# Output projection in three token passes, and the branch placed behind the first gather of a mixture-of-experts layer

## The reference, cut to what matters

```
x = x + merged @ w_out                       # merged: gated sum of the two mixers, (T, 2048)
h = rms_norm(x, g_ffn)
grp_prob = softmax(t @ w_router_group)       # 4 groups, top 1
g_p, g_i = top_k(grp_prob, 1)
sel_logits = router_expert logits of the chosen group        # 4 experts
e_p, e_i = top_k(softmax(sel_logits), 2)
w = g_p * (e_p / sum(e_p))
combine = sum(one_hot(expert_id, 16) * w)    # (T, 16)
hid = silu(t @ w_gate_e) * (t @ w_up_e)      # per expert, 512 wide
out = (hid * combine) @ w_down_e
y = x + out
```

## Time and profile before

| what | value |
|---|---|
| executions (3) | 1939.7, 1942.26, 2071.72 us |
| median | 1942.26 us |
| profiled execution | 1940.69 us |
| its span, slowest core (core 1) | 1939.1 us |
| spans of the 8 cores | 1922.6 to 1939.1 us |
| TensorE busy / VectorE busy / ScalarE busy | 86% / 42% / 38% of the span |
| projection, from first to last matmul (L1304) | 1207.6 to 1351.4 us |
| first matmul of the gather (L1464), of the experts (L1529) | 1407.85 us, 1433.26 us |

### The profile page before, as it was taken

One profiled execution on the slowest core, in us unless ns is written; L12 is line 12 of the kernel. 1 busy time (PEld: TensorE's weight loads), 2 busy tenths in 40 slices (PEclk: granted clock), 3 DMA queues, 4 the chain that ended last, 5 costly groups with the idle time before them and its releaser, 6 DMA issues.

```text
span 1939.1 us, 30864 instructions; the slowest of 8 cores (1922.6 to 1939.1 us)
## 1 busy us (share of the span) xinstructions
PE 1664.2 (86%) x11342; PEld 1072.2 (55%) x11342; DVE 820.7 (42%) x1244; ACT 743.0 (38%) x1246; POOL 143.5 (7%) x283
## 2 busy tenths in 40 slices
PE   2775777889998988879999999998588899898995
PEld 1542344566566566454444444887466676666662
DVE  3634334434434443421211212233435567665765
ACT  4654446556665655671111110032331322323221
POOL 0010100200201200001111100000000000010000
PEclk9887888899999999989999999999789999999997
DMA  9469891895995999546998972851139789798796
GB/s 255 170 101 115 104 122 23 105 115 68 121 113 70 123 121 117 114 66 110 138 121 120 141 98 53 245 122 66 25 71 244 163 208 234 179 216 207 193 236 212
DMA packets 57084, 263.09 MB, mean 136 GB/s; under 512 B 10464, under 2 KB 10720, under 8 KB 49312
## 3 DMA queue, kind: packets, MB, share of 16 engines
q0 software_dynamic: 27168, 152.06, 57.7%
q1 hardware_dynamic: 29760, 108.96, 17.2%
HBM read 404.65 MB, written 73.40 MB: 247 GB/s over the span
## 4 chain that ended last, share of the span: by engine, by line
PE 72%; DVE 9%; ACT 7%; issue 5%; DMA 4%; SPq 1%; DVEq 0%; ACTq 0%
PE psum L1116 11%; PE psum L586 11%; PE psum L1529 10%; PE psum L607 6%; PE psum L1121 6%; PE psum L1304 6%; PE psum L1565 5%; PE psum L933 4%; PE psum L915 4%; DMA arena<-wbf 3%; PE psum L1551 3%; PE psum L1464 2%; DVE arena L1473 2%; DVE arena L921 1%; DVE arena L559 1%
## 5 line engine op out<-in xcount | busy, mean ns | idle before, releaser
L586 PE MATMUL psum<-arena 128*128 128x512 bf16 (+1 forms) x1072 | 286.7, 403 | 13.6 <-DVE arena L559 13.5
L1529 PE MATMUL psum<-arena 128*128 128x256 bf16 x2048 | 243.7, 273 | 5.8 <-DMA arena<-wbf 5.8
L1529 PEld LDWEIGHTS psum<-arena 128*128 128x128 bf16 x2048 | 199.8, 98 | 55.9 <-issue 8.3
L1116 PE MATMUL psum<-arena 128*128 128x512 bf16 x1024 | 226.2, 379 | 0.0
L926 ACT ACTIVATE arena<-psum 128x512 bf16<-128x512 f32 x352 | 197.9, 592 | 34.8 <-PE psum L915 33.3
L933 PE MATMUL psum<-arena 128*128 128x256 bf16 x832 | 164.6, 280 | 49.9 <-ACT arena L923 41.9
L586 PEld LDWEIGHTS psum<-arena 128*128 128x128 bf16 x1072 | 106.8, 103 | 121.1 <-issue 50.9
L1116 PEld LDWEIGHTS psum<-arena 128*128 128x128 bf16 x1024 | 100.2, 98 | 120.6
L915 PE MATMUL psum<-arena 78*128 78x256 bf16 x832 | 166.0, 281 | 0.0
L1554 DVE TENSOR_TENSOR arena<-psum,arena 128x1024 f32<-128x1024 f32 x128 | 153.8, 1221 | 10.2 <-PE psum L1551 4.0
L559 DVE SCALAR_TENSOR_TENSOR arena<-psum,arena 64x512 bf16<-64x512 f32 (+3 forms) x121 | 89.4, 739 | 144.1 <-ACT arena L556 136.6
(11 more groups left out here) (152 smaller groups left out, 1831.1 us busy)
## 6 DMA issues: line engine op xcount, KB each, us to landing
wbf<-wexp POOLq DMA_DIRECT2D x108, 512.0 KB, 36.1
arena<-wbf SPq DMA_DIRECT2D x108, 512.0 KB, 12.6
arena<-wexp POOLq DMA_DIRECT2D x84, 512.0 KB, 10.5
arena<-win POOLq DMA_DIRECT2D x58, 512.0 KB, 9.3
arena<-xs SPq DMA_DIRECT2D x24, 1024.0 KB, 8.3
arena<-wobf SPq DMA_DIRECT2D x14, 1024.0 KB, 6.0
wobf<-wo POOLq DMA_DIRECT2D x8, 1024.0 KB, 57.4
arena<-wup POOLq DMA_DIRECT2D x16, 512.0 KB, 11.8
```

The costliest lines, as they stand in the source:

```text
L586: prog.add("pe", lambda e, k=k: e.matmul(PS(bank, 0, n), lhsT=wslot[s][:, k, :], rhs=src[:, k, lo:lo + n], start=(k == 0), stop=(k == 15)) ...
L1116: prog.add("pe", lambda e, k=k, bank=bank, wt=wt, tl=tl: e.matmul(PS(bank), lhsT=wt[:, k, :], rhs=hTo[:, k, tl:tl + 512], start=(k == 0), ...
L1529: prog.add("pe", lambda e, k=k, f=f, bank=bank, Wv=Wv: e.matmul(PS(bank, f * 256, f * 256 + 256), lhsT=Wv[:, k, :], rhs=X[:, k, e4 * 256:( ...
```

## The change

Four things are changed.

1. The projection has three passes: tiles 0 to 3, 4 and 5, 6 and 7. The slices are taken in the orders 0..7, 5 6 7 0..4 and 2..7 0 1, so each later pass begins with the three slices that the one before left. A third buffer `woslot[2]` lies on ring buffers 4 and 5. `load_wo` now names its buffer; 18 loads in all.
2. `side` holds tiles 0 to 5 (43 pieces, one of them a barrier), spread over the 32 groups of passes 1 and 2: `slot_no * nside / 31` says how many have to be out behind each group. Tiles 4 and 5 have scratch buffers of their own (`h2f_b`, `h2Tf_b`) on ring buffers 0 to 3. The tail holds tiles 6 and 7.
3. Since ring buffers 0 to 5 are in use, `load_slice(0..6)` is issued behind the last pass, behind a barrier; GpSimd's one-element copy is gone.
4. `build_P(0)` stands straight behind `pos`; the combine weights and their split come behind it, then `gather(0)` and `oprep(0)`, and only then the branch. The small routing tiles move out of the memory of `P` into that of `hid` for it.

```diff
-    B_wo = [Buf("wo%d" % i) for i in range(NWO)]
+    woslot.append(R3.alloc([128, 16, 256], BF16, at=16384))
+    B_wo = [Buf("wo%d" % i) for i in range(3)]
...
-    rt_small = [R3.alloc([128, 8, 16], F32) for _ in range(7)]
+    rt_small = [R3.alloc([128, 8, 16], F32, at=off_hidend - 4096 + i * 512) for i in range(7)]
...
+    h2f_b = R3.alloc([128, D], F32, at=0)
+    h2Tf_b = R3.alloc([128, 16, 128], F32, at=8192)
...
+    wo_seq = list(range(8)) + [0, 1, 2, 3, 4] + [5, 6, 7, 0, 1]
+    wo_at = {}
+
+    def load_wo(s):
+        if wo_seq:
+            n = wo_seq.pop(0)
+            wo_at[n] = s
+            prog.add("sp", lambda e: e.dma_start(out=woslot[s].rearrange("p a b -> p (a b)"), in_=wobf_d[n]),
+                     reads=[B_convo[3 if n < 4 else 7]], writes=[B_wo[s]], dsem=S_wo[s])
...
-    for t in range(4):
-        side.append(lambda t=t: part1(t, h2f_a, B_h2f_a))
+    for t in range(6):
+        hf, Bhf, hT_, BhT_ = (h2f_a, B_h2f_a, h2Tf_a, B_h2Tf_a) if t < 4 else (h2f_b, B_h2f_b, h2Tf_b, B_h2Tf_b)
+        if t == 4:
+            side.append(lambda: barrier([B_h2f_a], B_h2[4:6]))
+        side.append(lambda t=t, hf=hf, Bhf=Bhf: part1(t, hf, Bhf))
         if t:
-            side.append(lambda t=t: router(t - 1, h2Tf_a, B_h2Tf_a, 6))
-        else:
-            side.append(lambda: None)
+            hp, Bhp = (h2Tf_a, B_h2Tf_a) if t <= 4 else (h2Tf_b, B_h2Tf_b)
+            side.append(lambda t=t, hp=hp, Bhp=Bhp: router(t - 1, hp, Bhp, 6))
...
-    for pas in range(2):
+    for pas, (t_lo, t_hi) in enumerate(((0, 4), (4, 6), (6, 8))):
         nb = 8 if pas == 0 else 4
         for ci in range(8):
-            cg = ci if pas == 0 else (ci + 6) % 8
-            s = ci % NWO
-            for t4 in range(4):
-                t = pas * 4 + t4
+            cg = (ci + (0, 5, 2)[pas]) % 8
+            s = wo_at[cg]
+            for t in range(t_lo, t_hi):
...
-                if pas == 1 and side:
-                    side.pop(0)()
-            if pas == 1 or ci < 6:
-                load_wo()
+                if pas >= 1:
+                    slot_no[0] += 1
+                    while side and nside - len(side) < slot_no[0] * nside / 31.0:
+                        side.pop(0)()
+            if ci < 5:
+                load_wo(s)
...
-        if pas == 0:
-            prog.add("pool", lambda e: e.tensor_copy(out=flag_m[0:1, 0:1], in_=x1[0:1, 7, 0:1]),
-                     reads=[B_x1[7]], writes=[B_flag])
-            for i in range(7):
-                load_slice(i)
-    barrier(B_merged + [B_h2f_a, B_h2Tf_a], B_h2f + B_h2Tf + B_h2[4:8])
-    part1(4, h2f[0], B_h2f[0])
     while side:
         side.pop(0)()
-    for t in range(4, 8):
+    barrier([B_wo[2], B_h2f_b, B_h2Tf_b], B_ring[0:7])
+    for i in range(7):
+        load_slice(i)
+    barrier(B_merged + [B_h2Tf_a], B_h2f + B_h2Tf + B_h2[6:8])
+    part1(6, h2f[0], B_h2f[0])
+    for t in range(6, 8):
...
-    S_y = new_sem()
-    B_y = Buf("y")
-    prog.branch_at(flag_i[0:1, 0:1], B_flag)
-
...
+    build_P(0)
+    dv(lambda e: e.tensor_tensor(out=dsl, in0=sl, in1=l1.to_broadcast([128, 8, 4]), op=ALU.subtract))
+    prog.add("act", lambda e: e.activation(out=ex, in_=dsl, func=AF.Exp), reads=[B_rts], writes=[B_rts])
...
+    dv(lambda e: e.tensor_copy(out=wv[:, :, :, 2], in_=r2), R_, W_)
+    barrier([B_rts, B_wsp], [b for bb in B_hid for b in bb])
+    gather(0)
+    oprep(0)
+    S_y = new_sem()
+    B_y = Buf("y")
+    prog.branch_at(flag_i[0:1, 0:1], B_flag)
...
-    build_P(0)
-    gather(0)
-    oprep(0)
```

More of the change, by code:

```diff
@@ L1097, in build_program @@
     woslot = [R3.alloc([128, 16, 256], BF16) for _ in range(NWO)]
-    B_wo = [Buf("wo%d" % i) for i in range(NWO)]
-    S_wo = [new_sem() for _ in range(NWO)]
+    woslot.append(R3.alloc([128, 16, 256], BF16, at=16384))
+    B_wo = [Buf("wo%d" % i) for i in range(3)]
+    S_wo = [new_sem() for _ in range(3)]
     assert R3.off <= R3.size
-    barrier(all_attn_bufs, B_merged + B_sga + B_sgb + B_tmul + B_wo)
+    barrier(all_attn_bufs, B_merged + B_sga + B_sgb + B_tmul + B_wo[0:2])
     first = [True]
@@ L1178, in build_program @@
     B_L = Buf("L")
-    rt_small = [R3.alloc([128, 8, 16], F32) for _ in range(7)]
-    B_rts = Buf("rts")
     assert R3.off <= off_wo + 3 * 8192
@@ L1215, in build_program @@
     B_h2f_a, B_h2Tf_a = Buf("h2fa"), Buf("h2Tfa")
-    barrier(B_gs + B_sga + B_sgb + B_tmul, B_ring + [B_gbc2])
+    h2f_b = R3.alloc([128, D], F32, at=0)
+    h2Tf_b = R3.alloc([128, 16, 128], F32, at=8192)
+    B_h2f_b, B_h2Tf_b = Buf("h2fb"), Buf("h2Tfb")
+    barrier(B_gs + B_sga + B_sgb + B_tmul, B_ring + [B_gbc2, B_wo[2], B_h2f_b, B_h2Tf_b])
     barrier(B_attn_swa + B_attn_moba, B_h2 + [B_h2f_a, B_h2Tf_a])
     barrier(all_attn_bufs, [B_wr] + B_LT + [B_L, B_comb, B_M, B_pos, B_ones, B_wsp, B_flag, B_rts] + B_ss2l + B_sg + B_wsl)
[L1219 to L1227, removed]
-    load_wo()
-    load_wo()
+    wo_seq = list(range(8)) + [0, 1, 2, 3, 4] + [5, 6, 7, 0, 1]
[6 more added lines that the diff above has]
+                     reads=[B_convo[3 if n < 4 else 7]], writes=[B_wo[s]], dsem=S_wo[s])
+    load_wo(0)
+    load_wo(1)
     prog.add("sp", lambda e: e.dma_start(out=gbc2, in_=gffn_bc[:, :]), writes=[B_gbc2], dsem=S_gbc2)
@@ L1232, in build_program @@
              writes=[B_wr], dsem=S_wr)
+    load_wo(2)
     prog.add("dve", lambda e: e.memset(ss2, 0.0), writes=B_ss2l)
@@ L1280, in build_program @@
     side = []
[L1281 to L1282 removed]
+    for t in range(6):
[3 more added lines that the diff above has]
+        side.append(lambda t=t, hf=hf, Bhf=Bhf: part1(t, hf, Bhf))
         if t:
[L1284 to L1286 removed]
+            hp, Bhp = (h2Tf_a, B_h2Tf_a) if t <= 4 else (h2Tf_b, B_h2Tf_b)
+            side.append(lambda t=t, hp=hp, Bhp=Bhp: router(t - 1, hp, Bhp, 6))
         for q4 in range(4):
[L1288 removed]
+            side.append(lambda t=t, q4=q4, hf=hf, Bhf=Bhf, hT_=hT_, BhT_=BhT_: part2(t, q4, hf, Bhf, hT_, BhT_, 4 + q4 % 2))
         if t:
             side.append(lambda t=t: router_back(t - 1, 7))
[L1291 to L1292 removed]
+    side.append(lambda: router(5, h2Tf_b, B_h2Tf_b, 6))
+    side.append(lambda: router_back(5, 7))
+    nside = len(side)
+    slot_no = [0]
     ob2 = [0]
[L1294 removed]
+    for pas, (t_lo, t_hi) in enumerate(((0, 4), (4, 6), (6, 8))):
         nb = 8 if pas == 0 else 4
         for ci in range(8):
[L1297 to L1300 removed]
+            cg = (ci + (0, 5, 2)[pas]) % 8
+            s = wo_at[cg]
+            for t in range(t_lo, t_hi):
                 bank = ob2[0] % nb
@@ L1414, in build_program @@
              reads=[B_ps[0], B_M], writes=[B_pos])
[L1415 to L1435, removed]
-    S_y = new_sem()
-    B_y = Buf("y")
-    prog.branch_at(flag_i[0:1, 0:1], B_flag)
-    barrier(B_wo + B_merged + [B_gbc2, B_wr, B_L, B_rts, B_wsp] + B_LT + B_h2f + B_h2Tf,
-            B_X + [b for bb in B_Y for b in bb] + B_O + [B_P] + [b for bb in B_hid for b in bb] +
-            [B_wr] + B_LT + [B_L, B_rts])
+    barrier(B_wo + B_merged + [B_gbc2, B_wr, B_L, B_rts] + B_LT + B_h2f + B_h2Tf,
+            B_X + [b for bb in B_Y for b in bb] + B_O + [B_P])
     pb = [0]
```

24 lines of the change are left out of this document (20 added, 4 removed).

## The result

The changed kernel takes 1928.91 us in the median of 4 executions (1928.37 to 1930.53). Its ratio to the kernel before is 0.9939, 95% interval 0.9915 to 0.9963. Measured again on another occasion beside more executions of the kernel before (median 1938.65 of 11) it is 0.9932, interval 0.9914 to 0.995. So it is faster by 0.6%, some 12 us, which the interval tells apart from nothing. The forecast was 1931 us, 11.5 us under before. In some executions of these kernels the cores of one or both dies showed a lower granted clock and the time was up to 10% longer; ratios are taken from the others alone.

A forecast was written before the change was run, and what follows sets the result against it. TensorE's chain bounds the projection, short ScalarE and VectorE steps the tail and routing; what counts is how early the experts start. -7.3 + 11.5 + 2.9 - 15.5 - 3.1 = -11.5 us: forecast 1931 us, range 1920 to 1945.

The forecast's parts named there:

- the step from the sum to what a measurement would tell: Whole kernel: a measurement tells about 2% (39 us) from no change; within that 0.97, faster 0.01, slower 0.02.
- the wait at the first transposes: Start of pass 1: TensorE waits for VectorE's scaling of the first tile, +2.9 us; +4.6 if the clock drops too.
- The wait in pass 0: Projection, pass 0: the wait for a `w_out` slice goes once expert slices are issued later, -7.3 us.
- Rival C: Pass 0: residual tiles and `w_out` slices alone cause the wait, so it stays; time 1938, chance 0.08.
- The slices in passes 1 and 2: Passes 1 and 2: five slices loaded per pass land in time, 11.3 us available against 5.9 us; cost 0.
- Rival A: Passes 1 and 2: slices arrive too slowly and starve them, deciding from 6.8 us a load; slower than before, chance 0.07.
- Two more tiles: Projection passes: side work of two more tiles costs TensorE 5.75 us a tile, +11.5 us.
- The tail, -15.5: Tail behind the projection: two tiles instead of four take 20.5 us instead of 35.96, -15.5 us.
- The early gather, -8.3, the stop +3.5, the clock +1.7: Routing to experts: gather starts 8.3 us earlier, TensorE stops 3.5 us at the branch, then loses 1.7 to slow clock.
- Rivals B and D: Branch ahead of the experts: B, TensorE loses 11 us, time 1938, chance 0.12; D, it loses nothing, 1926, chance 0.12.
- My cancelling of the late weights against the table load: Gather: weights delay VectorE about 1.2 us, ScalarE's first copy loses a 1.28 us table load; length stays 25.4 us.
- The expert slices: Behind the projection: slices issued at about 1360 have some 60 us and need 18.9 us each; cost 0.

The follow-up runs named there:

- late_slices: The kernel before with one edit: the seven expert slices are issued behind the last pass instead of the first; ratio to the kernel before 0.9967.
- side_four: The changed kernel with side work for tiles 0 to 3 only, tiles 4 to 7 in the tail; ratio to the kernel before 0.9947.
- gap: The changed kernel with two empty pieces behind the first piece of side work, ahead of the first transposes; ratio to the kernel before 0.9914.
- passes_only: The changed kernel with its fourth part undone: combine weights and branch ahead of the one-hot again, three passes kept; ratio to the kernel before 0.9955.
- branch_only: The kernel before with the fourth part alone: one-hot behind the positions, weights beside the gather, branch behind it; ratio to the kernel before 0.9978.
- no_branch: The changed kernel without the branch and the second program, leaving out the case of an overflowing expert; ratio to the kernel before 0.9918.
- gap_busy_pe: The changed kernel with two empty pieces behind the first side work and 64 + 28 unread matmuls on TensorE during routing; ratio to the kernel before 0.9927.
- branch_after_onehot: The changed kernel with the branch between one-hot and gather and the combine weights spread over the gather; two executions, 1916.99 and 1923.11 us, no ratio.

## Why the prediction was right or wrong, step by step

The time (1931 forecast, 1928.9 measured, range 1920 to 1945) and the path to it came out as forecast, but two steps of the prediction failed.

The first is the step from the sum to what a measurement would tell. I put at 2% (39 us) the least change that can be told from none, with no row behind it, and so gave 0.97 to "within", although my own sum said 11.5 us. The interval of the ratio, 0.9915 to 0.9963, is 0.24% to either side and lies wholly under 1, and the second measurement has 0.9914 to 0.995: the change is a gain that can be told. The 2 to 3 us by which the fast executions shown before differed, which the prediction used for the lower end of its range, were the better measure.

The second is a term of the sum: the wait at the first transposes, +2.9, cost 4.7 us (step 3 below).

On core 1, from the first projection matmul to the first expert matmul, the change takes 12.25 us (225.7 to 213.4) off; the forecast for that way was 13.2.

1. *The wait in pass 0, -7.3.* Shown: pass 0 has no hole any more, and `late_slices` removes 7.0 us with that line alone. Rival C falls: without the expert slices the wait is gone on three cores and down to 0.2 to 0.6 us on four. Core 3 keeps 2.8 us, so a small part of the wait can have another cause on some core.
2. *The slices in passes 1 and 2, 0.* Shown on all cores of the changed kernel's profile. Ten loads landed in 4.9 us each, inside a window of 11.3:

```profile
arena<-wobf SPq DMA_DIRECT2D x10, 1024.0 KB, 4.9
```

Rival A decides from 6.8 us on, so it falls.

3. *Two more tiles, +11.5.* Shown by `side_four`, 11.4. *The wait at the first transposes, +2.9*: this is the term that was sized wrong. The wait itself was 2.94 us, but I took the clock to stay up behind it and kept the fall for the upper end of the range. On core 1 it falls, and `gap`, which takes the wait away, shows the step to cost 4.7 us. The upper end (4.6) was the right value there; on cores 0, 3 and 5 the clock stayed up, and the 2.9 was right.
4. *The tail, -15.5.* Measured -16.6, so this term was 1.1 short. I took the start of the old tail as it was; the second tile's transposes come 0.8 us sooner (11.2 us in, not 11.95), because ScalarE no longer has a third tile between them (in the kernel before it begins to square that tile at 1362.83, ahead of the second tile's first copy at 1365.41), and the two routers run without a break (64 passes in 7.17 us).
5. *The early gather, -8.3, the stop +3.5, the clock +1.7.* Shown: -8.3, +3.65 and +1.4 on core 1 (15.53 - 14.14), confirmed by `passes_only`, `branch_only` and `no_branch`. Rivals B and D fall with them: the branch costs TensorE what it cost VectorE, neither 11 us nor nothing. The rule of the Trainium skill that spoke against the change ("Runtime: NRT & Kernel Launch", Instruction fetch mechanics) fits the stop; that it is a fetch no run here shows. The 108 ns of "Advanced Engine Details and Errata", Control Flow Timing, is not what an engine loses here (3.65 us). My cancelling of the late weights against the table load also held on core 1: the gather itself, without the stop, is 28.94 - 3.65 = 25.3 us against 25.4 before. But `gap_busy_pe` shows that it held only because the clock was low.

The expert slices are the place where I was lucky rather than right. I gave them 60 us and a need of 18.9. Issued from 1361.7 on, and the last two from 1381.0, the nine of them took 12.2 us each to land (median) and kept the DMA engines busy to about 1391; the experts start at 1421, so the slack was some 30 us. Stretches of core 1:

```profile
1370.00:1380.00 10.00, 9.29 (x81) 8.52 (x79) 2.80 (x7) 5.02 (x5) 0.00 (x0) 1.00 1.03 179
...
1380.00:1390.00 10.00, 0.42 (x3) 0.24 (x3) 5.97 (x33) 0.23 (x1) 1.07 (x2) 0.65 1.03 191
...
1390.00:1395.00 5.00, 2.85 (x14) 2.03 (x15) 3.50 (x10) 1.12 (x2) 0.00 (x0) 0.50 0.14 30
```

The terms of core 1 add up: the projection +9.1 (-7.3 + 11.5 + 4.7 = +8.9), the tail -16.6, to the gather -8.3, gather and stop +3.5, the experts -0.1: -12.4, and the span fell by 12.3. The experts' 1.4 us of slow start are in the -0.1, so something else there is 1.5 us shorter; over the 8 cores that stretch scatters by several us from run to run (496 to 508 in the twelve profiles), and I have no cause for it. There is luck in how close the sum came: the projection cost 2.0 us more than forecast (9.1, not 7.1), and against it stand 1.1 us in the tail and 1.8 in the experts' stretch (-0.1, where I had +1.7), the latter without a known cause.

## What to carry to other kernels

When work is taken out of a tail and woven into a loop, write down behind which instruction each piece falls: the pieces cost what they cost, but one consumer too close to its producer gave back more than half of what the move had earned, and two empty pieces brought it back. A branch on a value computed on the device cost TensorE and VectorE 3 to 5 us each here, so put it where the engine that sets the time is waiting anyway; and when a wait on a transfer is found, look first at what else was issued in the same microseconds before adding buffers.

## What the runs showed of the hardware that I had not expected

- A wait of 2.94 us can be enough for TensorE to come back at its lower clock level and lose another 1.7 us, but it does not on every core: it did on 5 of 8 in the changed kernel and on 30 of 40 over the five runs with this wait. Behind the wait of 2.27 us with which the projection starts in all twelve profiles, the granted clock of the next 1.5 us was under 0.95 on 20 of 96 cores. After 1.19 us (`side_four`) it fell on none of eight. Behind the stop at the branch the loss was 1.4 to 2.1 us on all eight cores of the changed kernel.
- A branch costs TensorE 3.2 to 3.7 us in the changed kernel (eight cores), about what it cost VectorE in the kernel before (3.5 to 4.2). With the branch behind the one-hot (`branch_after_onehot`), where TensorE stands idle before it, 4.75 us pass on core 1 between the flag and the first matmul.
- A faster TensorE made a stretch slower: started at full clock it reached a wait that the lower clock had hidden, and that wait took the clock away again.
